# A decoder step with its list of chosen blocks six cycles sooner, two samples' rows fetched by GpSimd, and the sliding rows moved up on SyncE's queue

## What is computed

```python
kc = compress_blocks(kv_cmp, pe, w1, w2)             # 127 compressed keys for a sample
p = masked_softmax(q @ kc[..., 0], cmask)
imp = einsum('bgrtn,nj->bgtj', p, overlap)           # what each block of 64 tokens is worth
rank = where(valid, imp + BIG * forced, -BIG)        # block 0 and the last two are forced
_, idx = lax.top_k(rank, 16)
kvg = ks[bi, gi, idx]                                # rows of the 16 chosen blocks, by head group
o_sel = softmax(q @ kvg_keys) @ kvg_values
o_win = window_attn_dense(q, last 512 rows + new row)   # the sliding cache
out = (g0 * o_cmp + g1 * o_sel + g2 * o_win, o_a) @ w_out
```

## Time and profile before

| | us |
|---|---|
| median of 3 runs | 2688.13 (2686.74 to 2691.56) |
| profiled execution, its own time | 2688.47 |
| its span in the trace | 2686.9 |
| TensorE busy with matmuls in the span | 2559.3 (95%) |
| VectorE, GpSimd, ScalarE busy | 1497.4, 1454.3, 927.3 |
| SP's transfer issues in the chain that ended last (L3168, its queue) | 4.4% of the span |

### The profile page before, as it was taken

How to read it: one execution, slowest core, us unless ns; L and a number is a source line. 1 busy time by engine, 2 the same in 40 slices (tenths; PEclk the granted TensorE clock), 3 DMA queues, 4 the chain that set the end, 5 groups by cost and what they waited for, 6 DMA issues and landing times.

```text
span 2686.9 us, 51959 instructions
## 1 busy us (share of the span) xinstructions
PE 2559.3 (95%) x21231; PEld 2468.6 (92%) x21231; DVE 1497.4 (56%) x1955; ACT 927.3 (35%) x1607; POOL 1454.3 (54%) x955
## 2 busy tenths in 40 slices
PE   8999989998996499999999999999999999999998
PEld 8999978987775399999999999999999999999998
DVE  5112385877663016655567667537337545577676
ACT  4100044656674105333334334311124333334342
POOL 6332201121322154877788885643558777798881
PEclk9999999999998699999999999999999999999999
DMA  6112353342012432435465442321222444563431
GB/s 199 48 26 88 94 153 106 95 155 83 16 33 64 136 119 103 163 114 166 143 222 200 144 154 64 126 64 48 95 103 103 150 127 154 201 237 123 154 127 64
DMA packets 221766, 319.91 MB, mean 119 GB/s; under 512 B 37069, under 2 KB 152530, under 8 KB 217882
## 3 DMA queue, kind: packets, MB, share of 16 engines
q1 hardware_dynamic: 214176, 307.08, 34.4%
q10 hardware_dynamic: 6442, 8.46, 1.0%
q0 software_dynamic: 912, 1.05, 0.2%
HBM read 224.83 MB, written 95.90 MB: 119 GB/s over the span
## 4 chain that ended last, share of the span: by engine, by line
PE 80%; SPq 7%; DVE 5%; POOL 3%; issue 2%; DMA 1%; ACT 1%; ACTq 0%; DVEq 0%; POOLq 0%
PE psum L933 19%; PE psum L957 19%; PE psum L484 16%; PE psum L532 7%; SPq L3168 4%; PE psum L976 3%; PE psum L2320 2%; SPq L3167 2%; PE psum L2313 1%; POOL whl L397 1%; PE psum L520 1%; PE psum L2293 1%; PE psum L2787 1%; PE psum L3719 1%; PE psum L2817 1%
## 5 line engine op out<-in xcount | busy, mean ns | idle before, releaser
L957 PE MATMUL psum<-part_hi,whl 128*128 128x258 f32 x3136 | 507.7, 284 | 0.8 <-POOL whl L397 0.5
L957 PEld LDWEIGHTS psum<-part_hi,whl 128*128 128x128 f32 x3136 | 434.2, 189 | 1.4 <-POOL whl L397 0.7
L454 POOL TENSOR_TENSOR whl<-wraw,zeroc 128x1024 fp32r<-128x1024 f32 x62 | 119.5, 1927 | 424.4 <-PE psum L484 171.4
L484 PE MATMUL psum<-xhi,whl 128*128 128x344 f32 x1776 | 329.2, 320 | 2.1 <-DVE qT L1676 1.0
L933 PE MATMUL psum<-shi,whl 128*128 128x258 f32 x1920 | 323.9, 283 | 0.0
L1240 DVE TENSOR_TENSOR xlo_plain<-xlo_plain,psum 128x516 f32<-128x516 f32 x360 | 244.9, 688 | 140.8 <-PE psum L957 138.5
L957 PE MATMUL psum<-part_lo,whl 128*128 128x258 f32 x1568 | 315.0, 282 | 0.0
L484 PEld LDWEIGHTS psum<-xhi,whl 128*128 128x128 f32 x1776 | 288.2, 188 | 2.6 <-issue 2.6
L933 PEld LDWEIGHTS psum<-shi,whl 128*128 128x128 f32 x1920 | 271.4, 190 | 0.0
L933 PE MATMUL psum<-xhi,whl 128*128 128x258 f32 x1440 | 247.4, 284 | 7.2 <-POOL whl L365 4.1
L957 PEld LDWEIGHTS psum<-part_lo,whl 128*128 128x128 f32 x1568 | 243.1, 190 | 0.0
(11 more groups left out here) (553 smaller groups left out, 5209.8 us busy)
## 6 DMA issues: line engine op xcount, KB each, us to landing
part_raw<-b_spill SPq DMA_DIRECT2D x98, 516.0 KB
b_spill<-rows_H SPq DMA_DIRECT2D x78, 516.0 KB, 4.2
rows<-in_cache_cmp_kv SPq DMA_DIRECT2D x128, 128.0 KB, 2.7
raw_even<-in_w_ffn SPq DMA_DIRECT2D x16, 1024.0 KB, 5.9
out_even<-in_w_ffn SPq DMA_DIRECT2D x16, 1024.0 KB, 6.1
out_odd<-in_w_ffn SPq DMA_DIRECT2D x16, 1024.0 KB, 6.0
raw_odd<-in_w_ffn SPq DMA_DIRECT2D x14, 1024.0 KB, 7.2
wraw<-in_w_in_ab SPq DMA_DIRECT2D x26, 512.0 KB, 4.7
```

The costliest lines, as they stand in the source:

```text
L454: pool.tensor_tensor(whl[:, s, 0, :], raw, zeroc[:, 0:1].to_broadcast([P, UNIT]), ALU.add).then_inc(w_hi, 1)
L484: last = pe.matmul(psum[:, 3 * bset + c, 0:TC], w, rhs[ah][:, k0 + k, c * TC:(c + 1) * TC], start=(k == 0 and n == 0), stop=(k == kn - 1 a ...
L957: last = pe.matmul(psum[:, 2 * p + h, 0:QT], out_weights(first, n, wh)[:, k, p % 2, :], (part_hi, part_lo)[ah][x][:, k, h * QT:(h + 1) * Q ...
```

## The change

Three things are moved.

```diff
-        SAMPLE_STEPS = ((2, 3), (2, 7), (3, 5), (3, 8), (4, 5), (5, 3))
+        SAMPLE_STEPS = ((2, 3), (2, 7), (3, 5), (3, 8), (4, 3), (5, 3))
...
-                if c == cycle_of(sample_step(3)) + 6:
+                if c == cycle_of(sample_step(3)) + 5:
                     act_compressed_exp(act)
...
-                if c == cycle_of(sample_step(3)) + 8:
+                if c == cycle_of(sample_step(3)) + 6:
                     dve_compressed_probs(dve)
+                if c == cycle_of(sample_step(4)) + 4:
+                    dve_block_sums(dve)
+                if c == cycle_of(sample_step(4)) + 4:
+                    dve_block_ranks(dve)
                 if c == cycle_of(sample_step(4)) + 5:
-                    dve_block_sums(dve)
-                if c == cycle_of(sample_step(4)) + 7:
-                    dve_block_ranks(dve)
-                if c == cycle_of(sample_step(4)) + 9:
                     dve_block_choice(dve)
...
             for b in range(5):
-                chosen_rows(sp, b)
+                chosen_rows(sp, b, (0, 1))
             sp.wait_ge(p_ql, 2 * NT)
-            sp.wait_ge(p_qk, soft_no[job_no[("c", NT - 1, 0)]] + 1)
-            forced_rows(sp, 5)
             sp.wait_ge(p_qk, soft_no[job_no[("s", NT - 1, HB - 1)]] + 1)
             window_rows(1)
-            chosen_rows(sp, 5)
+            forced_rows(sp, 5)
+            chosen_rows(sp, 5, (0,))
             new_rows(1)
             sp.wait_ge(p_qk, len(SOFT))
             window_rows(2)
             window_rows(3)
-            forced_rows(sp, 6)
-            chosen_rows(sp, 6)
+            chosen_rows(sp, 5, (1,))
             new_rows(2)
             new_rows(3)
...
-            forced_rows(pool, 7)
-            chosen_rows(pool, 7)
+            for b in (6, 7):
+                forced_rows(pool, b)
+                chosen_rows(pool, b, (0, 1))
```

More of the change, by code:

```diff
@@ L3159, in forced_rows, with chosen_rows @@
                 .then_inc(rows_sem(b), 16)
-        def chosen_rows(eng, b):
-            for g in range(2):
+        def chosen_rows(eng, b, groups):
+            for g in groups:
                 r = HB * b + 4 * g
```

## The result

| | before | changed |
|---|---|---|
| median, us | 2689.85 (2686.74 to 2692.32, 4 runs) | **2649.48** (2647.69 to 2650.44, 4 runs) |
| ratio, 95% interval | | 0.985, 0.9833 to 0.9867 |
| span of the profiled execution | 2686.9 | 2648.8 |
| TensorE busy in it | 2559.3 | 2557.0 |

The account below looks back on a forecast made before the run. SP's queue of issues was taken as the bound. The list 12.9 us sooner and 29.9 us from sample 6 leaving SP put w1's keys 42.8 us sooner, for a median of 2645.3 us, range 2640 to 2652.

Parts of the forecast that it names:

- The bound: SP's queue from 704.7 to 910.7 us: 182 issues at about 1.05 to 1.08 us each cost the time, not the data.
- Rival 3: SP's queue: transfers, not issues, set the pace, so only the earlier list gains; 2675.2 us, chance 0.03.
- The earlier list: Sample choice on VectorE: list written earlier, so SP's first issue moves from 704.7 to 691.8 us, 12.9 us sooner.
- just such a stall: VectorE ahead of the list: a stall in the probabilities and step 4 could eat 2 us of the gain.
- Sample 6 leaves SP: End of SP's queue: 30.36 us spent on sample 6 go, less 0.5 for one more start, 29.9 us.
- The sliding rows first: SP's order: w0's wait of 26.19 us goes nearly whole, worth nothing on its own, but covers w1's 2 MB windows.
- What stays: TensorE's waits for new sliding rows: some 12 us remain at w1, under 2 us at w0; SP still the bound.
- GpSimd's second sample: GpSimd's queue: sample 7 follows sample 6, issues end by 875.2, landing at 877.3 against a need at 881.4; hidden.
- Rivals 2 and 5: GpSimd's queue: its transfers grow or land late, 2666 us, chance 0.08; it fills and waits for room, 2696, chance 0.05.
- Behind w1: After w1's keys: reload and output product move along unchanged, 26.5 us from w1's keys to the first L3539.
- The clock: TensorE's speed after the wait at w1: no gain given; some 2 us if the clock stayed up, otherwise zero.
- The sum: From SP's first issue to w1's keys 176.1 us, so w1's keys start at 867.9 instead of 910.7, 42.8 us sooner.

Follow-up runs that it names:

- e6: Changed kernel with each of the 13 transfers of SP's first chosen group split into two halves, 26 issues for the same bytes: 2661.62 us, ratio 0.989.
- e3: Changed kernel with sample 6 put back on SP's queue behind sample 5's second group, GpSimd having sample 7 alone: 2678.98 us, ratio 0.995.
- e4: Changed kernel with SP's old order: both groups of sample 5 ahead of the new row of wrow[1] and w1's windows: 2656.92 us, ratio 0.9865.
- e5: Changed kernel with sample 5's second group also given to GpSimd, ahead of samples 6 and 7: 2650.2 us, ratio 0.9858.
- e2: Changed kernel with the list's steps put back where they were before, the new queues kept: 2659.08 us, ratio 0.9884.
- e8: Changed kernel with steps 2, 3 and 4 of the samples moved further up, to tile 3 places 2, 5 and 11: 2649.19 us, ratio 0.9851.
- e7: Changed kernel with seven of the 13 transfers of sample 5's second group issued behind w1's new rows: 2642.74 us, and 2643.14 us when run again.

## Why the forecast held, and where it was off

- **The bound.** SP's issues, not the transfers: held. DMA rows for 705 to 820 us, to set beside the earlier trace rows:

```profile
q1 hardware_dynamic: 15264, 3.48, 13.8%
...
srows<-in_cache_sel_kv SPq DMA_DIRECT2D x107, 32.0 KB, 2.2
```

  The same share and landing, and e6 puts a price on 13 issues without a byte more. Rival 3 is out.
- **The earlier list: 12.9 forecast, 11.7 measured** (31.57 - 19.86). This is the term that was mis-sized. The order was as forecast, two of its durations were not the earlier trace rows:

```profile
688.27 0.82 DVE L2930 TENSOR_REDUCE nmax<-psum 128x1 f32<-128x640 f32 x1 [0.71 <-PE psum L2761]
689.01 0.27 DVE L3344 TENSOR_REDUCE rank<-pg 64x32 f32<-64x128 f32 x1
689.31 0.73 DVE L3345 TENSOR_TENSOR rank<-rank,pg 64x32 f32<-64x32 f32 x1
...
694.06 0.17 DVE L3361 TENSOR_SCALAR chosen<-top 64x16 int32<-64x16 f32 x1
```

  The maximum ahead of the sums waited 0.71 us for TensorE, whose step 4 (L3265, 0.43 us) and longer transposes (1.07 us instead of 0.73) now stand ahead of its scores; and an addition took 0.73 us instead of 0.21. Together 0.71 + 0.52 = 1.2 us. The forecast had kept 2 us for just such a stall. In the traces the first issue came at 694.7 instead of the forecast 691.8: 1.2 of it are these, 1.7 the later attention of this execution.
- **Sample 6 leaves SP: 29.9 forecast, 30.7 in e3.** Held, and for the whole chain 206.0 - 176.5 = 29.5.
- **The sliding rows first: "worth nothing on its own" in the kernel with sample 6** holds in e3. It was named as cover and never priced; e4 gives the price, 6 to 7 us. Without it the forecast sum would have been too good by as much.
- **What stays.** 12 us of wait at w1 were forecast, 13.9 measured, for `wrow<-kv_scratch`. w0's was to be under 2 and is 1.34 (2.21 when the changed kernel was profiled again).
- **GpSimd's second sample.** Forecast to be done by 875.2; the last issue starts at 875.05 and ends at 875.58. That it came so close is partly luck: GpSimd started 1.5 us later than before, and the gap ahead of sample 7 was 1.20 us and not 2.19. The issues are 0.95 us apart to the last. Rivals 2 and 5 are out, and the trap ahead of them is seen in e5: with 13 more it is late at once.
- **Behind w1.** 26.88 us to the output product, 26.5 forecast; 0.35 us lost.
- **The clock.** No gain was given, and there is none on the path:

```profile
853.00:858.00 5.00, 2.96 (x50) 2.09 (x44) 0.95 (x3) 1.88 (x5) 2.95 (x6) 1.00 0.77 215
...
863.00:868.00 5.00, 0.00 (x0) 0.00 (x0) 0.00 (x0) 0.00 (x0) 2.64 (x5) 0.50 0.77 102
868.00:873.00 5.00, 1.82 (x8) 1.57 (x8) 0.00 (x0) 0.60 (x1) 2.65 (x5) 0.50 0.21 48
873.00:878.00 5.00, 5.00 (x53) 2.97 (x52) 0.95 (x3) 1.86 (x4) 1.58 (x3) 0.67 0.16 30
878.00:883.00 5.00, 5.00 (x72) 3.55 (x65) 1.29 (x2) 3.34 (x8) 0.00 (x0) 1.00 0.77 251
```

  After 13.88 us of waiting TensorE was granted 0.50, the 1.2 GHz level, as after 28.31; in the last row it is back at full speed. At w0, after a wait of only 1.34 us, it had stayed up (first row), and TensorE's work there took 2.1 us instead of 3.8; the wait at w1 swallowed that.
- **The sum.** 11.7 + 29.5 = 41.2, less 0.35 behind w1, makes 40.9 from the maximum to the output product, against 42.8. The profiled executions differ by 2688.47 - 2650.44 = 38.0, since tile 4 came 1.7 us later and the part behind the output product took 1.0 longer (1750.7 and 1749.7), where nothing was changed. The median, 2649.48, lies 4.2 us above the forecast 2645.3: 2.4 are missing gain, and 1.7 come from the median before, which is 2689.85 here and was 2688.13 in the three runs the forecast started from.

## What to carry to other kernels

Where small transfers with addresses from a register stand on one queue, count issues, not bytes, and look for a second engine that issues at the same pace. Splitting one group into twice the issues for the same bytes shows which of the two it is (it does not tell an issue's price from that of the rows in it). When the last such group leaves a queue, look at what it had covered: here the landing of a large load that the next instruction waits for. A few issues put into the hole cost little (six about 2 us instead of 6), while more than fill it delay what follows. And measure parts against a mark just ahead of the edit, since the start of the stage scattered over 9 us from run to run.

## What the runs showed of the hardware

**A VectorE operation held up by one of GpSimd.** The addition of 64x32 values took 0.21 us before and 0.73 in the changed kernel, ending at 690.04. GpSimd at that time:

```profile
687.73 0.88 POOL L2675 TENSOR_SCALAR pbuf<-pbuf,wgt,gates 128x640 f32<-128x640 f32 x1 [1.60 <-DVE wgt L2960]
688.69 1.28 POOL L2666 TENSOR_TENSOR qhl<-qB,qhl 64x512 fp32r<-64x512 f32 x1
```

It ended at 689.97, and the addition right behind. In all ten traces with this order of VectorE the addition took 0.72 to 0.76 us, and 0.21 in both with the old one (before, e2). In e8 the addition was clear of such an operation and took 0.21 again, while a comparison took 0.95 instead of 0.17, until GpSimd's next one was over:

```profile
691.86 1.04 POOL L2661 TENSOR_TENSOR qhl<-qB,zeroc 64x512 fp32r<-64x512 f32 x1
```

```profile
688.93 0.21 DVE L3345 TENSOR_TENSOR rank<-rank,pg 64x32 f32<-64x32 f32 x1
...
691.98 0.95 DVE L3356 TENSOR_SCALAR ckey<-rank 64x32 f32<-64x32 f32 x1
```

The Trainium skill (SBUF — State Buffer, section SBUF: two separate sides) says that VectorE and GpSimd share a pair of ports, and that whichever starts first of a GpSimd operation and a VectorE operation with two inputs in SBUF, or in a two-port mode, holds the pair for its whole instruction. By that rule the price is what is left of GpSimd's operation, and these two rows agree. The addition has two inputs, `rank` and `pg`; the comparison has one, and whether it is in such a mode no row shows. The sum at 689.01, with one input, and the maximum at 688.27, which reads PSUM, ran beside GpSimd's operations at 687.73 and 688.69 without growing.

**Landing depends on what else is in flight.** GpSimd's transfers of 32 KB landed after 2.1 us. In the changed kernel it was a median of 5.7 between 851 and 862 us, beside the two windows, and 2.1 again between 862 and 876; in e5 it was 6.7 between 870 and 893, beside reload and weights:

```profile
srows<-in_cache_sel_kv POOLq DMA_DIRECT2D x22, 32.0 KB, 6.7
```

Their issues stayed 0.95 us apart all the while. In e7 the last was issued at 874.07, and TensorE's wait for it ended at 881.88.
